# Grouped rows of the expert weights: one 4 KB piece per partition, and a strided stationary operand in the gather

## The reference, cut to what matters

```
for e in range(N_EXPERTS):
    y = (silu(t @ w1[e]) * (t @ w3[e])) @ w2[e]
    out = out + gates[:, e:e + 1] * y
```

## Time and profile before

| what | value |
|---|---|
| median of 3 runs (lowest to highest) | 907.45 us (906.88 to 909.03) |
| the profiled execution's own time | 907.71 us |
| its span, first to last instruction | 905.8 us |
| mean granted TensorE clock | 0.961 |
| TensorE matmul busy | 833.9 us, 92% of the span |
| DMA | 300.59 MB, 332 GB/s on average |
| expert stage of layer 0, first to last expert matmul | about 232 to 482 us |
| expert stage of layer 1 | about 646 to 892 us |

### The profile page before, as it was taken

One profiled execution on the slowest core, in us unless ns is written; L12 is line 12 of the kernel. 1 busy time (PEld: TensorE's weight loads), 2 busy tenths in 40 slices (PEclk: granted clock), 3 DMA queues, 4 the chain that ended last, 5 costly groups with the idle time before them and its releaser, 6 DMA issues.

```text
span 905.8 us, 16815 instructions
## 1 busy us (share of the span) xinstructions
PE 833.9 (92%) x6940; PEld 520.8 (57%) x6940; DVE 406.6 (45%) x674; ACT 241.3 (27%) x449; POOL 93.1 (10%) x162
## 2 busy tenths in 40 slices
PE   5898999999999799999996999989899899998994
PEld 2588995596646355553543887467555355453541
DVE  0468998737422222332336643466622232332334
ACT  3742435613211011111103523343111111110112
POOL 4184000012000000000000254100000000000000
PEclk9999999997999799999997999999999899999998
DMA  9999996848999999989997986596999999989993
GB/s 357 367 259 295 333 355 192 289 164 286 368 392 397 392 397 391 389 274 399 394 398 294 328 240 184 172 382 225 385 391 397 389 398 393 392 304 393 392 397 131
DMA packets 142158, 300.59 MB, mean 332 GB/s; under 512 B 12576, under 2 KB 43584, under 8 KB 142072
## 3 DMA queue, kind: packets, MB, share of 16 engines
q1 hardware_dynamic: 135360, 286.53, 87.5%
q0 software_dynamic: 6384, 12.76, 4.9%
q10 hardware_dynamic: 328, 0.11, 0.0%
HBM read 291.77 MB, written 2.92 MB: 325 GB/s over the span
## 4 chain that ended last, share of the span: by engine, by line
PE 66%; DMA 17%; DVE 8%; issue 3%; ACT 3%; SPq 2%; DVEq 0%; ACTq 0%
PE ps L2016 20%; DMA ring<-in_moe_w 11%; PE ps L2041 11%; PE ps L1969 4%; DMA ring<-in_w_mod 4%; PE ps L2106 3%; PE ps L1939 3%; DMA ring<-in_na_w_in 2%; PE ps L1940 2%; PE ps L1620 2%; PE ps L2132 2%; PE ps L2134 2%; PE ps L2133 2%; SPq L621 2%; DVE wlo L1106 2%
## 5 line engine op out<-in xcount | busy, mean ns | idle before, releaser
L2016 PE MATMUL ps<-ring,xg 128*64 128x256 f32 (+1 forms) x2432 | 255.3, 394 | 11.1 <-DMA ring<-in_moe_w 9.7
L2016 PEld LDWEIGHTS ps<-ring,xg 128*64 128x64 f32 (+1 forms) x2432 | 134.3, 130 | 103.2 <-issue 41.2
L1475 DVE SCALAR_TENSOR_TENSOR xres<-ps,gs,xres 128x512 f32<-128x512 f32 x128 | 90.0, 747 | 188.4 <-PE ps L1969 188.4
L2041 PE MATMUL ps<-ring,hidT 128*64 128x512 f32 (+1 forms) x608 | 121.8, 607 | 7.5 <-DMA ring<-in_moe_w 6.7
L2041 PEld LDWEIGHTS ps<-ring,hidT 128*64 128x64 f32 (+1 forms) x608 | 33.0, 129 | 76.6 <-issue 63.2
L1106 DVE TENSOR_TENSOR wlo<-ring,whi 128x1024 fp32r<-128x1024 f32 x56 | 66.6, 1219 | 12.8 <-ACT whi L807 12.8
L807 ACT CAST whi<-ring 128x1024 fp32r<-128x1024 f32 x56 | 56.8, 1045 | 53.0 <-DMA ring<-in_na_w_in 37.0
L1459 DVE TENSOR_TENSOR yg<-ps,g2keep 128x512 f32<-128x512 f32 x32 | 21.5, 689 | 82.7 <-PE ps L2041 82.7
L1620 PE MATMUL ps<-ring,pair 128*32 128x256 f32 x576 | 45.6, 436 | 12.6 <-DMA ring<-in_w_mod 7.7
L974 ACT COPY xg<-ps 128x384 f32<-128x384 f32 (+2 forms) x44 | 20.7, 470 | 130.7 <-PE ps L1940 130.7
L1939 PE MATMUL ps<-pick,hthi 128*128 128x192 f32 (+1 forms) x192 | 50.3, 302 | 0.0
(11 more groups left out here) (265 smaller groups left out, 1323.7 us busy)
## 6 DMA issues: line engine op xcount, KB each, us to landing
ring<-in_moe_w SPq DMA_DIRECT2D x384, 512.0 KB, 11.7
ring<-in_w_mod SPq DMA_DIRECT2D x96, 512.0 KB, 7.3
ring<-in_na_w_in SPq DMA_DIRECT2D x24, 512.0 KB, 8.7
ring<-in_cf_pw_w SPq DMA_DIRECT2D x24, 512.0 KB, 8.4
ring<-in_ab_w_out SPq DMA_DIRECT2D x8, 512.0 KB, 4.9
mods<-mod_scratch POOLq DMA_DIRECT2D x8, 512.0 KB, 7.1
urep<-uT SPq DMA_DIRECT2D x64, 35.5 KB, 3.5
urep<-uT POOLq DMA_DIRECT2D x64, 35.5 KB, 3.4
```

Source lines behind the costliest of these rows:

```text
L1475: V.scalar_tensor_tensor(out=dst, in0=ps[:, plan.spread_banks(m, i)[half], :], scalar=gs[:, t, place:place + 1], in1=dst, op0=ALU.mult, op ...
L2016: ins = T.matmul(ps[lo:lo + width, BW[a], c0:c0 + 2 * P], tile[:, k, o:o + width], raw[:, p.slot(u), w0:w0 + 2 * P], start=(q == 0 and kk ...
L2041: ins = T.matmul(ps[lo:lo + width, BY[a], :], hidT[:, a, o:o + width], raw[:, p.slot(u), half * HALF:(half + 1) * HALF], start=(q == 0), s ...
```

## The change

The rows of w1 and w3 are dealt out to partitions the other way: partition p takes rows 8p to 8p + 7, and unit q takes two of them, 8p + 2q and 8p + 2q + 1, which lie next to each other in HBM. The half kk of unit q on partition p is now row 8p + k with k = 2q + kk. For the sum to meet the same row of the tokens, the gather takes for block k the columns k, k + 8, k + 16, ..., 128 of them.

```diff
                 if name == "w2":
                     src = src[0, q * P:(q + 1) * P, :]
                 else:
-                    src = src[0].rearrange("(k p) n -> p k n", p=P)[:, 2 * q:2 * q + 2, :]
-                    dst = dst.rearrange("p (k n) -> p k n", k=2)
+                    src = src[0].rearrange("(p k) n -> p (k n)", k=KC)[:, 2 * q * FF:(2 * q + 2) * FF]
                 eng.dma_start(dst, src).then_inc(p.landing(u), 16)
...
                                 sel = pick[:, t, first:first + turns, 0, :]
-                                T.matmul(dst, hthi[:, t, k * P:(k + 1) * P], sel, start=(t == 0), stop=False)
-                                ins = T.matmul(dst, htlo[:, t, k * P:(k + 1) * P], sel, start=False, stop=(t == NT - 1))
+                                T.matmul(dst, hthi[:, t, k:D:KC], sel, start=(t == 0), stop=False)
+                                ins = T.matmul(dst, htlo[:, t, k:D:KC], sel, start=False, stop=(t == NT - 1))
```

## The result

The changed kernel takes 938.69 us (median of its comparison; 907.16 for the kernel before beside it). The ratio is 1.0333, with a 95% interval of 1.0293 to 1.0373: 3.3% slower. The ratio leaves out one of the four runs of the changed kernel, a slow one of 955.1 us at a mean granted clock of 0.938; the quotient of the medians, which holds it, is 1.035. The profiled execution took 938.02 us, of which its span is 936.2 us, 30.4 us more than before. The forecast was 891; Rival A, the strided load that costs double, stood at 925.

What follows compares the result with a forecast made beforehand. The prediction took the weight-unit stream as the limit in two stretches of each expert stage and PE elsewhere there. It took 12.3 us of waits plus 4.2 us of low clock, 16.5 us, off to reach 891 us, range 887 to 925.

Steps and rivals of the forecast that it cites:

- Rival A: Gather: the strided load takes twice as long, 42.2 us more for PE, net 17.6 us, 925 us; chance 0.30.
- The four limited stretches: Two per expert stage (225-313, 411-476, 640-726, 822-887 us), where the stream of weight units, not PE, is the limit.
- 16.2 us of waits: PE's waits for weight units in the expert stages: 5.7, 2.6, 4.2 and 3.7 us; 3.9 us expected to remain.
- Part one: w1/w3 units in 4 KB pieces: 0.07 us saved on each of 176 units, 12.3 us, plus 4.2 us of clock.
- the clock: PE's low granted clock after waits in three stretches of the stages costs 8.4 us; half, 4.2 us, was counted as gain.
- Part two: The gather's 384 weight loads with a stride of eight columns: price taken as 0, doubling kept as a rival.
- a reserve of 0.045 us a step: Gather: loads follow at 0.11 us, but columns can be delivered at 0.066 us each load; the difference may absorb the stride.
- the row that I used against Rival A: Transposes of dwsort: 17 loads of 128 four-byte columns in 1.12 us, 0.066 us each, matmuls included.
- The cover: What a slower gather fills before it shows: 16.2 us of waits and 8.4 us of low clock, 24.6 us.
- the break-even of 0.175 us: Gather step, 0.064 us more a load over 384 loads, at which the kernel is where it was; beyond is slower.
- Rival B: Gather: the strided load loses a little, up to 0.05 us, eating the stream's gain; 891 to 902 us; chance 0.12.
- Rival C: Weight stream: pieces still split, or the 16 KB distance cancels the gain; units stay at 1.355 us, 907 us; chance 0.08.

Runs made afterwards that it cites:

- row_pairs2: Repeat of row_pairs, the same kernel profiled again: 897.0 us against 908.9 for the kernel before, ratio 0.9848.
- half_strided: The changed kernel with only the high part's gather load strided, the low part written sorted and loaded contiguously: 917.68 us, ratio 1.0113.
- row_pairs: The changed kernel, but each partition takes rows 2p and 2p + 1 of the unit's own 256, gather stride two columns: 896.8 us, ratio 0.9866.
- stride_right: The kernel before with its 2 KB pieces, gather stride of eight, copies written scattered so tokens route as before: 944.26 us, ratio 1.0411.

## Why the prediction was wrong

**What bounds the kernel: right.** The four limited stretches are where both effects showed. Of the 16.2 us of waits that the prediction counted the strided gather filled 12.5.

**Part one: about right in the stages, not in the whole.** The unit saves 0.075 us for the 0.07 taken, with pieces 16 KB apart. Without the slow load the stages are 13.5 to 16.8 us shorter for the 16.5 forecast. The split was off: I put 12.3 us on waits and 4.2 on the clock. In row_pairs2 8.4 us of the waits went and 7.8 remain where I expected 3.9, and the low clock was gone altogether, not by half. That the sum came out is in part luck, for the two misses cancel. And even with a free load the forecast of 891 would have been 6 us too low, inside its own range of 887 to 899 but near the end: the best kernel takes 897, since the parts outside the stages, which the forecast left as they were, came out 5.8 to 8.2 us longer in the profiles.

**Part two: the step that failed.** "The gather's load has a reserve of 0.045 us a step, and that may absorb the stride. I take 0". The cost that I put at 0 had to be 0.128 us x 384 = 49.2 us: the step between loads went from 0.112 to 0.240 us. The reserve of the earlier trace rows is real: a load over twice as many 16-byte stretches, stride 2, costs only 0.006 us more. But I compared columns, and the row counts something else. Its 128 columns lie side by side on 32 stretches of 16 bytes, 0.066 us; a stride of eight columns touches 128, four times as many. Scaled by four the same row gives an estimate of 0.26 us a load, a tenth above the 0.240 measured. (Its loads are 8 partitions high, but those of line 1990 in the same trace are 128 x 128 as in the gather; there the second of two loads starts 0.058 us after the first, and four times that is 0.23.) So the row that I used against Rival A could have priced it. The Trainium skill's page Advanced Engine Details and Errata, section Memory Cachelines, had named the unit in which to count; I set its rule aside because it has no price, though the earlier trace rows gave one to work from.

**Rival A: right in kind, short in size.** Its signs came: a step above 0.2 us, SP waiting longer, and a DMA share below 1, though only in the first limited stretch of each stage. It gave 925 for a measured 938.7. Two terms were off. The price was 42.2 us and is 49.2 (0.128 for 0.11; the ceiling was a load at the low clock, which has another cause). The cover was 24.6 us and is 19.2, of which 12.5 are waits (16.2 less the 3.7 that remain): some waits stay, and the low clock does not go with them as the rival had it. With both the rival's sum is 30.0 us, and the span is 30.4 longer. That the cover does not reach the first gathers, 64 of the loads, changes nothing in this sum, because the loads in the stages alone cost more than the cover. It does change the break-even of 0.175 us, as half_strided shows. In the stages 41.0 less 19.2 is 21.8 us (the 19.2 is itself read from them). Outside, 64 loads at 0.128 us would be 8.2 us. The two first gathers took 6.7 us longer, less than that because in the kernel before a part of them lies at the low clock, at 0.21 us a step. There the clock rises at about 228 us, within the gather; in the changed kernel it stays at 0.50 until about 240, four us into the stage.

**Rival B**, a small price of up to 0.05 us, did not come for the change; the 0.006 us of row_pairs are of its kind. **Rival C** falls: 32,766 packets are gone, and units of the new pieces land at 414 GB/s.

**The range.** 925 was the end because the doubling was "the far end". A doubling was the nearest row, not a bound, and nothing in the trace kept the load below it.

## What to carry to other kernels

Before giving a load a stride, count how many 16-byte stretches of SBUF it touches, not how many elements; two float32 columns on each were nearly free for TensorE's weight load here (0.118 us for 0.112), one on each doubled it (0.233 to 0.240). A stride that a layout in HBM forces may be made smaller by regrouping within the transfer: here rows in pairs gave the same 4 KB pieces and kept the gain. And when two effects of a change draw on the same waits, add up the waits once, and set aside the part of the cost that lies outside the stages that have them (here 64 of 384 loads).

## What the runs showed that I had not expected

- The strided load takes 0.240 us a step at a granted clock of 0.50 and of 1.00 alike, while the contiguous one takes 0.21 and 0.11. That reads as two limits, one that goes with TensorE's clock and one that does not; no run shows what either of them is.
- Strides 4 to 8 cost nearly the same, 0.227 to 0.240 us, with 5 and 6 the lowest.
- Alternating loads do not keep their own prices: the strided one is followed after 0.217 us instead of 0.240 and the contiguous one after 0.131 instead of 0.112; the sum, 0.348, is that of the two (0.352).
- ACT and DVE pay for a stride as well. Reading every eighth float32, a copy of 128 x 1024 takes 2.08 us instead of 1.06 on ACT and the subtraction 2.02 instead of 1.22 on DVE; written with that stride instead (stride_right), it is 2.08 and 2.02 again.
- A stretch at 0.77 or 0.78 of the clock (150 to 180 us), before anything that was edited, in three of the profiles; its cause is open.
